# The first norm on rows of x, the second half of the rows issued by ScalarE's queue as its first instruction

## What is computed

```python
def rmsnorm(x, g):
    xf = x.astype(jnp.float32)
    y = xf * lax.rsqrt(jnp.mean(xf * xf, axis=-1, keepdims=True) + EPS) * g.astype(jnp.float32)
    return y.astype(x.dtype)
...
        h = rmsnorm(x, attn_pre_norm[l])
        proj = h @ w_in[l]
```

## Time and profile before

| what | us |
|---|---|
| median of 3 runs | 1043.69 (1043.69 to 1044.56) |
| the profiled execution | 1042.57 |
| its span, first to last instruction | 1040.8 |
| PE busy in it | 1024.4 (98%) |
| DVE busy | 804.5 (77%) |
| ACT busy | 592.5 (57%) |
| POOL busy | 165.4 (16%) |
| HBM read | 225.19 MB, 219 GB/s over the span |

### The profile page before, as it was taken

The page is one execution under the profiler, slowest core; times in us unless marked ns, Lnnn a source line. Parts: engine busy times, 40 slices in busy tenths (PEclk is TensorE's granted clock), DMA queues, the critical chain, the costliest instruction groups (busy, mean ns, idle before and its releaser), DMA issues.

```text
span 1040.8 us, 19237 instructions
## 1 busy us (share of the span) xinstructions
PE 1024.4 (98%) x7860; PEld 974.9 (94%) x7860; DVE 804.5 (77%) x1378; ACT 592.5 (57%) x1027; POOL 165.4 (16%) x172
## 2 busy tenths in 40 slices
PE   8999999999999999999999999999999999999997
PEld 7988898999889997999999999988999999999997
DVE  5877799999997977588999788885678576674443
ACT  5688676666446766665444455443465566544443
POOL 1000134333102100032212011201100123111010
PEclk8999999999999999999999999999999999999999
DMA  9733356776894433457998787653435546774441
GB/s 364 266 117 123 122 195 243 282 285 248 342 401 146 157 126 118 188 191 275 377 370 308 288 322 271 202 196 127 163 122 186 179 142 235 280 260 148 168 168 41
DMA packets 34132, 227.49 MB, mean 219 GB/s; under 512 B 3795, under 2 KB 4092, under 8 KB 10492
## 3 DMA queue, kind: packets, MB, share of 16 engines
q1 hardware_dynamic: 33596, 223.63, 58.9%
q0 software_dynamic: 448, 2.63, 0.6%
HBM read 225.19 MB, written 2.63 MB: 219 GB/s over the span
## 4 chain that ended last, share of the span: by engine, by line
PE 87%; DVE 9%; ACT 2%; issue 1%; DMA 1%; POOL 0%; SPq 0%; POOLq 0%; ACTq 0%; DVEq 0%
PE psum L1506 21%; PE psum L1508 21%; PE psum L1507 21%; DVE w_lo L2258 3%; PE psum L1571 2%; PE psum L1574 2%; PE psum L1573 2%; PE psum L1922 2%; PE psum L1924 2%; PE psum L1923 2%; PE psum L1713 1%; ACT w_hi L820 1%; DVE arena L2582 1%; PE psum L1868 1%; PE psum L1605 1%
## 5 line engine op out<-in xcount | busy, mean ns | idle before, releaser
L2258 DVE TENSOR_TENSOR w_lo<-raw,w_hi 128x1024 fp32r<-128x1024 f32 (+2 forms) x340 | 387.3, 1160 | 143.5 <-ACT w_hi L820 137.8
L820 ACT ACTIVATE w_hi<-raw 128x1024 fp32r<-128x1024 f32 (+2 forms) x340 | 333.4, 996 | 210.3 <-PE psum L1508 155.7
L1506 PE MATMUL psum<-h_hi,w_hi 128*128 128x256 f32 (+1 forms) x1144 | 324.3, 283 | 5.1 <-DVE w_lo L2258 2.6
L1508 PE MATMUL psum<-h_hi,w_lo 128*128 128x256 f32 (+1 forms) x1144 | 320.1, 280 | 0.0
L1507 PE MATMUL psum<-h_lo,w_hi 128*128 128x256 f32 (+1 forms) x1144 | 319.9, 280 | 0.0
L1506 PE MATMUL psum<-hid_hi,w_hi 128*128 128x256 f32 (+1 forms) x952 | 270.9, 285 | 0.5 <-DVE w_lo L2258 0.4
L1507 PE MATMUL psum<-hid_lo,w_hi 128*128 128x256 f32 (+1 forms) x952 | 268.1, 282 | 0.0
L1508 PE MATMUL psum<-hid_hi,w_lo 128*128 128x256 f32 (+1 forms) x952 | 268.1, 282 | 0.0
L1506 PEld LDWEIGHTS psum<-h_hi,w_hi 128*128 128x128 f32 x1144 | 214.8, 188 | 8.5 <-DVE w_lo L2258 5.1
L1507 PEld LDWEIGHTS psum<-h_lo,w_hi 128*128 128x128 f32 x1144 | 215.7, 189 | 0.7 <-issue 0.7
L1508 PEld LDWEIGHTS psum<-h_hi,w_lo 128*128 128x128 f32 x1144 | 215.2, 188 | 0.0
(11 more groups left out here) (297 smaller groups left out, 1221.2 us busy)
## 6 DMA issues: line engine op xcount, KB each, us to landing
arena<-in_ada SPq DMA_DIRECT2D x48, 1024.0 KB, 6.6
raw<-in_gu SPq DMA_DIRECT2D x44, 1024.0 KB, 6.7
raw<-in_ret_in SPq DMA_DIRECT2D x24, 1024.0 KB, 4.9
raw<-in_up SPq DMA_DIRECT2D x22, 1024.0 KB, 4.9
raw<-in_dn SPq DMA_DIRECT2D x32, 704.0 KB, 4.2
raw<-in_qkv SPq DMA_DIRECT2D x12, 1024.0 KB, 5.0
raw<-in_down SPq DMA_DIRECT2D x11, 1024.0 KB, 7.9
raw<-in_ret_o SPq DMA_DIRECT2D x8, 1024.0 KB, 4.9
```

The lines of the kernel that those rows point to most:

```text
L820: nc.scalar.activation(w_hi[chunk % SPLIT_SLOTS][:, a:b], raw[chunk % RAW_SLOTS][:, a:b], ACT.Copy)\
L1506: nc.tensor.matmul(out, w[0], hc, start=start, stop=False, skip_group_check=True)
L1508: return nc.tensor.matmul(out, w[1], hc, start=False, stop=stop, skip_group_check=True)
L2258: tt(w_lo[s][:, a:b], raw[chunk % RAW_SLOTS][:, a:b], w_hi[s][:, a:b].bitcast(F32), ALU.subtract)\
```

## The change

x comes to SBUF a second way: `x_rows`, with the 256 rows of x on the partitions (row r*128 + p on partition p, half r in columns r*1024 and on), 1 MB in two halves. Half 0 is SP's first DMA; half 1 is ACT's first instruction. The squares are summed along the free axis (ACT with `accum_out`, DVE with one `tensor_tensor_reduce` per half), the factor is a number per partition, and the rows are scaled by it (ACT one 512-column piece, DVE three). PE transposes the scaled rows, two 128x128 blocks per tile k, into five PSUM banks in turn (`turn_x`). ACT makes `h_hi` from PSUM with the gain as scale, DVE makes `h_lo` from PSUM, gain and `h_hi`. POOL has no part in it now. The first weight quarter of 512 columns is loaded and split by itself; the order of the three matmuls of a product changes, so that the one that needs `h_lo` is last. Matmuls on `busy` are left only once (20 of them). The old layout of x is still needed for the residual much later; SP loads it (1 MB, one DMA) behind chunk ROWS0 (step 4 of `w_in`), and DVE waits for it (`x_in`) ahead of the second norm.

```diff
+            sp.dma_start(x_rows[:, 0:D], dram["x_rows"][:, 0:D]).then_inc(x_rows_in[0], 16)
-            sp.dma_start(onehot, dram["onehot"]).then_inc(onehot_in, 16)
-            for (a, b), landed in ((PH["w_in"].halves(LAT0)[0], first_in), (PH["w_in"].halves(LAT0)[1], raw_in[0])):
+            for a, b, landed in ((0, 512, first_in[0]), (512, 1024, first_in[1]), (1024, 2048, raw_in[0])):
+                if a == 512:
+                    sp.dma_start(onehot, dram["onehot"]).then_inc(onehot_in, 16)
                 sp.dma_start(raw[0][:, a:b], dram["w_in"][0:P, a:b]).then_inc(landed, 16)
...
+                    if ph.name == "w_in" and step.j == 4:
+                        sp.dma_start(x[:, :], dram["x"]).then_inc(x_in, 16)
...
-            odd_rest(1)
-            odd_rest(3)
             pool.wait_ge(band_out, 16)
             pool.dma_start(dram["band_rows"], dram["band_repeat"]).then_inc(band_out, 16)
-            odd_rest(5)
-            odd_rest(7)
...
+            act.dma_start(x_rows[:, D:2 * D], dram["x_rows"][:, D:2 * D]).then_inc(x_rows_in[1], 16)
...
+            for r in range(2):
+                act.wait_ge(x_rows_in[r], 16)
+                nc.scalar.activation(row_part(row_h, r, 0), row_part(x_rows, r, 0), ACT.Square, scale=D ** -0.5,
+                                     accum_out=row_stat[:, 28 + r:29 + r]).then_inc(pre_sq, 1)
...
+            def turn_x(k):
+
+                for r in range(2):
+                    if r == 0 and k < 4:
+                        pe.wait_ge(pre_first_row, 1)
+                    else:
+                        pe.wait_ge(pre_rows, 1 if k < 4 else 2 + r)
+                    ins = nc.tensor.transpose(turned_x(k)[:, r * P:(r + 1) * P], row_h[:, r * D + k * P:r * D + (k + 1) * P], ident[:, :])
+                ins.then_inc(pre_turned, 1)
...
+            for r in range(2):
+                dve.wait_ge(x_rows_in[r], 16)
+                own = row_part(x_rows, r, 1)
+                ins = nc.vector.tensor_tensor_reduce(row_part(row_h, r, 1), own, own, 1.0 / D, 0.0, ALU.mult, ALU.add,
+                                                     row_stat[:, 30 + r:31 + r])
...
+            for r, n in ((1, 0), (0, 1), (1, 1)):
+                ts(row_part(row_h, r, n), row_part(x_rows, r, n), scales[:, r:r + 1], 1.0, ALU.mult, ALU.mult).then_inc(pre_rows, 1)
...
+            for k in range(DT):
+                if k % 2 == 0:
+                    first_quarter(k // 2)
+                cut = slice(k * S, (k + 1) * S)
+                dve.wait_ge(pre_hh, k + 1)
+                stt(h_lo[:, cut], turned_x(k), col("pre", k), h_hi[:, cut].bitcast(F32), ALU.mult, ALU.subtract).then_inc(pre_tiles, 1)
```

More of the change, by code:

```diff
@@ L768, in _ @@
             for i in range(len(NORM_GROUPS)):
[L769 removed]
+                if NORM_GROUPS[i]:
                     add_squares(i)
@@ new lines, in _ @@
+            act.wait_ge(first_in[0], 16)
+            first_quarter(0)
+            act.wait_ge(cols_in, 16)
+            round_turned(0)
+            round_turned(1)
+            act.wait_ge(first_in[1], 16)
+            first_quarter(1)
+            round_turned(2)
+            round_turned(3)
+            act.wait_ge(raw_in[0], 16)
+            first_quarter(2)
+            act.wait_ge(band_ps, 1)
+            nc.scalar.activation(band, sco[0][0:8, 0:BAND], ACT.Copy).then_inc(band_ready, 1)
@@ L1634, in _ @@
             pe.wait_ge(busy_ready, 1)
-            keep_busy(20)
-            pe.wait_ge(ones_filled, 1)
-            sums(PRE)
+            keep_busy(20, lin[1])
+            pe.wait_ge(ident_in, 16)
+            def turn_x(k):
[6 more added lines that the diff above has]
+                ins.then_inc(pre_turned, 1)
+            turn_x(0)
+            turn_x(1)
             pe.wait_ge(cols_in, 16)
             pe.wait_ge(onehot_in, 16)
[L1641 to L1644, removed]
+            nc.tensor.matmul(sco[0][0:8, 0:BAND], col("rel", 0, 8, BUCKETS + 1), onehot, start=True, stop=True).then_inc(band_ps, 1)
+            turn_x(2)
+            turn_x(3)
             def bank_free(unit):
@@ L1649, in bank_free, with features @@
                 return lin[unit % 2]
[L1651 to L1656, removed]
+            def features(ph, c, bank, nb, kt, rhs=(h_hi, h_lo), first_tiles=None, hooks={}, whole=True):
+                whi, wlo = weights(ph.chunk0 + c, Step(c), ph)
                 cut2, blocks, half_at = ph.halves(c)[1][0] // P, nb * kt, 0
@@ L1678, in features, with first_features @@
                         ins.then_inc(half_done, 1)
+            def first_features(bank):
+                for k in range(DT):
+                    if 0 < k < 5:
+                        turn_x(k + 3)
+                    t = slice(k * S, (k + 1) * S)
+                    for b in range(2):
+                        at, q = 2 * k + b, k // 2
+                        cut, out = slice(at * P, at * P + P), bank[:, b * S:(b + 1) * S]
+                        if at % 4 == 0:
+                            pe.wait_ge(hi_ready if q % 2 else first_hi, q // 2 + 1)
+                        if b == 0:
+                            pe.wait_ge(pre_hh, k + 1)
+                        nc.tensor.matmul(out, w_hi[0][:, cut], h_hi[:, t], start=at == 0, stop=False, skip_group_check=True)
+                        if at % 4 == 0:
+                            pe.wait_ge(split_ready if q % 2 else first_lo, q // 2 + 1)
+                        nc.tensor.matmul(out, w_lo[0][:, cut], h_hi[:, t], start=False, stop=False, skip_group_check=True)
+                        if b == 0:
+                            pe.wait_ge(pre_tiles, k + 1)
+                        ins = nc.tensor.matmul(out, w_hi[0][:, cut], h_lo[:, t], start=False, stop=at == 2 * DT - 1, skip_group_check=True)
+                        if at in (DT - 1, 2 * DT - 1):
+                            ins.then_inc(half_done, 1)
             def value_rows(c, after):
@@ L2313, in rest_of @@
                         ins = stt(lo_[:, cut], tmp[:, cut], shift(k), hi_[:, cut].bitcast(F32), ALU.add, ALU.subtract)
-                    ins.then_inc(h_tiles, 2 if i == PRE else 1)
-                def then(k):
-                    if i != PRE or k % 2 == 0:
-                        rest_of(k)
-                    if i == PRE and k in (1, 3):
-                        first_quarter(2 + k // 2)
-                scale_tiles(i, then)
+                    ins.then_inc(h_tiles, 1)
+                scale_tiles(i, rest_of)
             def norm_h(i, meanwhile=None):
```

108 lines of the change are left out of this document (47 added, 61 removed).

## The result

| | before | this |
|---|---|---|
| median of the runs beside each other, us | 1043.72 (22 runs) | 1045.24 (22 runs) |
| fastest and slowest, us | 1041.90, 1046.74 | 1043.28, 1049.07 |
| profiled execution, us (span) | 1042.57 (1040.8) | 1047.82 (1046.0) |

The ratio is 1.0018, with a 95% interval of 1.0009 to 1.0026: slower by some 1.9 us (the medians differ by 1.5), where 3.3 off was forecast.

What follows compares the result with a forecast made beforehand. PE, busy 98% of the span, was taken as the bound; its product stream reaching LAT1 3.5 us earlier, less 0.2 lost behind, gives 3.3 off: 1043.69 to 1040.4 us, range 1038.7 to 1042.4.

Steps and rivals of the forecast that it cites:

- The start: Kernel start up to LAT1: factor at 8.35, first product at 10.2, LAT1 at 18.8, 3.5 us earlier than 22.34.
- the rule weighed in the prediction: Landing of the rows: several issuing engines save only issue time; second half at 5.95, the sum some 0.4 us less.
- The clock: PE's clock in the first chunk: half from about 11, rising near 15.0, with LAT1 starting at 18.8.
- The same fall at about 11.1 is likely: First chunk: PE's clock falls to half near 11.1, as before, since PE has gaps from 7.7 to 10.2.
- the rival of a clock that never falls: First chunk: DVE is the bound, LAT1 at 17.2, the bias table leaves 4.1 us off; 1039.6 us, chance 0.15.
- What comes behind: Feeders behind LAT1, mainly the bias table and ROWS0: PE keeps the 3.5 us lead less 0.2 us.
- the table lands at 39.55 + 0.8 = 40.4: Bias table's DMA chain: starts 0.8 later, lands at 40.4; DVE wants it at 40.1, PE loses from 41.0 on.
- I take 0.2 us lost there: Loss allowed behind the start for the later bias table and x's 1 MB on SP's queue: 0.2 us.
- SP's queue was never empty beside them either: Argument against a late bias table: its two large DMAs ran beside loads on SP's queue before too.
- said to land at 31.0 as before: ROWS0's weight load: lands at 31.0, wanted at 30.1, its split waiting under 1 us, using up only slack.
- the bias table comes late: Rival: two large table DMAs each stretched 2.7 us, landing 45.8, PE 1.3 later than before; 1045.0 us, chance 0.05.
- 0.9 us to spare: Kernel before, at PE's transposes: DVE's last step ends at 49.26, PE gets there at 50.13, 0.9 us spare.

Runs made afterwards that it cites:

- e4: The change with the second half of the rows issued by SP right behind the first, no DMA on ACT's queue; ratio 0.9999 to before.
- e6: The kernel before, with x loaded a second time (1 MB, read by nobody) where the change loads it; ratio 0.9994 to before.
- e1: The change with the 1 MB load of x moved from behind ROWS0 to behind the second chunk of w_out; ratio 0.9987 to before.
- e5: The change with x late, the one-hot table ahead of the columns, the band chain early, and the second ada piece behind ROWS1; ratio 0.9976 to before.
- e7: The change with only the second piece of ada (1 MB) issued behind ROWS1 instead of ahead of ROWS0; ratio 1.0008 to before.
- e10: The change with 28 instead of 20 matmuls on busy at the start and nothing else; ratio 1.0002 to before.
- e2: The change with the band matmul ahead of the first transposes and its copy behind the first scaled piece, x left in place; ratio 0.9989 to before.
- e3: The change with x loaded late and the band matmul and its copy moved early; ratio 0.9985 to before.
- e8: The change without the band repeat and skewed read, one plain 1 MB weight load in the table's place, bias not computed; ratio 0.9983 to before.
- e9: e5 with 28 instead of 20 matmuls on busy and six more behind the first eight transposes; ratio 0.9983 to before.

## Why the prediction was wrong

**The start was right.** The halves landed at 5.6 and 5.8 (forecast 5.5 for both), the mean squares were there at 7.04 (7.0), the factor at 8.22 (8.35). The first product came at 10.83 (10.2), because PE waited 1.4 us for ACT's scaled piece and had all eight transposes behind that. Nobody missed POOL's four tiles. By the rule weighed in the prediction (the Trainium skill, DMA: Bandwidth & Descriptors, Issuing engines are not separate DMA queues) the second half would land at 5.95, 0.4 earlier than with one issuing engine. The traces agree within their spread: where ACT issues the second half, the halves landed at 5.5 to 5.9 and 5.7 to 6.1 (nine kernels, one execution each), and where one engine issues both, at 5.1 to 5.2 and 6.4 to 6.5 (before, e4, e6). So the second half won about 0.5, and the first lost as much, which the prediction had allowed for.

**The clock** was neither right nor wrong. "The same fall at about 11.1 is likely" didn't happen in the profiled execution of the change, where products ran 0.12 apart at once and the rival of a clock that never falls gave the better start (LAT1 17.2 forecast there, 17.57 measured). In e1 and e4 products were 0.21 apart until about 16, and in e5 between 11.8 and 15, much as forecast, with leads of 1.5 to 2.6. The Trainium skill (TensorE: Matmul & The Clock Gate, Part 4: PE-mode transpose) would have the transposes keep the full clock from engaging. The change's trace can't test that, since its clock was full from 8.1, ahead of the first transpose at 9.12; it shows that the transposes didn't bring the clock down again and themselves ran 0.11 apart there, against 0.22 at half clock in e1. Why the same instructions started at one level or the other stays open.

**The step that failed is "What comes behind"**: "the table lands at 39.55 + 0.8 = 40.4", and of x's megabyte "I take 0.2 us lost there". The chain did start 0.7 later, as reckoned. But the table landed at 45.0, and at 45.3, 45.4 and 46.0 in e4, e7 and e10, which kept both the megabyte and the late start. The term that was mis-sized is the megabyte: 3.3 us on the table's landing by e6, which adds it to the kernel before and nothing else (42.9 against 39.6), instead of 0.2. In the new form e4 and e1 are the closest pair, with the table issued at 31.5 and leads of 1.5 and 1.7: 45.3 with x and 41.6 without, 3.7. The mistake in the reasoning was "SP's queue was never empty beside them either": the engines being full already is no ground for nothing to happen. Some other load has to wait for an added megabyte, by some 2.7 us in all (an estimate: 1.05 MB at the 385 GB/s of the earlier trace rows), and the table, which ends late in the full stretch, is a likely payer. The Trainium skill (DMA: Bandwidth & Descriptors, Issuing engines are not separate DMA queues) says that DMAs of all issuing engines run on the same 16 DMA engines and interleave; the sums above are what that means here, with the table on POOL's queue and x on SP's. It isn't always the table that pays: with its chain early, e2 with x and e3 without have it at 42.1 and 42.2. There the loads behind x on SP's queue paid: ROWS1, MLA and QA1 landed at 37.4, 40.6 and 43.2 with x, and at 32.9, 34.7 and 39.7 without.

The rest, up to 45.0, is 45.0 - 40.4 - 3.3 = 1.3 us that were not reckoned with. They lie in the second DMA of the chain, the repeat into `band_rows`: it took 12.9 in the change against 11.5 before and in e6, while the last DMA took 12.9 in the change and 13.1 in e6. An earlier PE frees buffers earlier, and the loads follow: ROWS0 was issued at 14.7 instead of 18.1, x at 15.1, and ROWS1 at 18.7, beside the repeat (18.9), instead of 23.5. The repeat took 13.2 in e10, with the same quick start, but 10.7 and 11.7 in e4 and e7, with x and a slower one. A kernel with a quicker start thus seems to push its own chain back; that these loads are the cause was argued, not tested alone.

**ROWS0** was said to land at 31.0 as before, with the split waiting under 1 us. It landed at 33.4 and ACT waited 4.5. That cost PE some 3.4 us of lead on the way (4.8 to 1.4), but it doesn't set the end: e4 and e7, without that wait, were as late at the transposes, and e8, e1 and e5, without the late table, kept their leads. Two waits in a row each ate the same lead; to remove the first alone gives it to the second. The quick start with ROWS0 late and the table in time was not run; by these numbers 1.4 of the lead would be left.

**The rival that came true** is "the bias table comes late". It named the mechanism (each of the two large DMAs stretched by 2.7 us), the place, the landing (45.8; measured 45.0 to 46.0), and 1.3 behind before (measured 0.8 at the transposes, 1.1 at the mark). Its chance of 0.05 was the error. That the landing came out so near is in part luck: the last DMA was stretched by 2.9, the repeat only by 1.4, and not at all in e6. By the rule read off the runs (PE's transposes = landing + 5.7, where the table is late: 42.1 to 47.81, 42.2 to 47.91, 45.0 to 50.73, 45.3 to 51.04, 45.4 to 51.12, 46.0 to 51.72), a table behind 44.2 makes the kernel slower than before. (The prediction took PE's transposes at 50.13 and had 0.9 us to spare behind DVE; the first of them starts at 49.97, so it was 0.7.) The kernel before had 43.60 - 39.6 = 4.0 us of spare time in this DMA. The change took 0.7 + 3.3 of that by itself, and drew in other loads besides.

**What stays open.** The measured 1.9 us exceed the 1.1 of the mark by 0.8. From the mark to the end the profiled executions take 935.9 us before, 936.4 in e6, and 938.2 to 940.6 in the ten kernels of the new form. Nearly all of this excess lies in two stretches in which PE waits for nothing and the granted clock is 1.00, and yet products start 0.120 apart instead of 0.118. In 510 to 570 PE has 502 or 503 matmuls in all ten, against 511 and 512 in before and e6, and the stretch around it costs 2.3 us; in 190 to 250 it has 502 in seven of them, the change among them, against 511 or 512 in the others, 1.5 us. No cause was found. The timed runs can't all carry it: e5's profiled execution has both stretches, and its ratio still gives 2.5 us off, as much as its mark. The ratios follow the marks within about 2 us: e4 and e10 came out 1.5 and 1.9 better than their marks, and e9 1.5 worse. By groups they agree with the bound: the four kernels with the table at 45.0 or later have 0.9999 to 1.0018, the six others of the new form 0.9976 to 0.9989. Whether the ratio of the change and that of e4 (1.0018 and 0.9999, intervals that just touch) differ for a reason is open too; their profiles show the same bound.

## What to carry to other kernels

Where a start is to be made quicker, list every DMA that is issued in the busy stretch behind it, on all queues, with its landing and the time at which it is wanted; a megabyte that is added there can fall in full on the one that ends last (3.3 us here), and the lead shortens the spare time of all of them. A load that nobody needs for a long while belongs behind the last one that is needed soon: moving x alone turned 1.0018 into 0.9987, and with the chain of the table started early, and one more load moved back, into 0.9976.

## What the runs showed of the hardware

A DMA that is issued earlier can land later. ROWS0's load, 776 KB on SP's queue, was issued at 14.72 in the change and landed at 33.4; in e4 it was issued at 18.05 and landed at 30.5, with the same loads ahead of it in the queue (QA0's landed at 23.6 and 22.1, the second piece of `ada` at 29.3 and 25.4). The moved bytes per second were the same, 422 and 418 GB/s in 14 to 19, so it looks as if the engines shared their time among the queued loads in another way; how, no run here tells.

A granted clock of 1.00 at the start of a trace need not be a full clock. In e1 the view gives 1.00 for 12 to 16 while products ran 0.21 apart, the spacing that goes with half the clock before (granted 0.5 from 11.1 to 17.9):

```profile
13.00 0.41 PE L1703 MATMUL psum<-h_hi,w_hi 128*128 128x256 f32 x1
13.21 0.41 PE L1706 MATMUL psum<-h_hi,w_lo 128*128 128x256 f32 x1
```

```profile
12.00:16.00 4.00, 4.00 (x21) 4.00 (x20) 2.09 (x4) 2.25 (x5) 0.71 (x1) 1.00 1.04 425
```

The trace of e1 has its first record of the clock at 15.9, where the spacing goes to 0.12, and the view counts time without a record as full. In the change the first record stands at 8.1. Ahead of the first record the spacing of like products is the reading to use.
